# Twelve of branch four's forty filling pieces move from branch three's steps to branch four's own first six

## The reference

```
proj = h @ w_in          # queries, keys, values of all branches
o_a = diff_attention(aq, ak, av, ...)      # branches one and two of the kernel, 2 heads each
o_b = dilated_attention(bq, bk, bv, ...)   # branch three
o_c = dsa_attention(cq, ck, cv, iq, ik, iw, ...)  # branch four, keys chosen by an indexer (top 256)
x = x + concat(o_a, o_b, o_c) @ w_out
h = rmsnorm(x, norm_mem)
x = x + memory_attention(h, rmsnorm(mem, norm_memkv), w_mq, w_mkv, w_mo)
```

## Time and profile before

| | before |
|---|---|
| median of 3 runs (range) | 3524.21 us (3521.84 to 3525.72) |
| profiled execution, its span | 3520.07 us, 3518.2 us |
| PE busy, DVE busy, ACT busy | 96%, 49%, 28% |
| chain that ended last | PE 86%, DVE 7%, ACT 4% |
| steps 32 to 47 (branch three) | 192.73 us, PE busy 192.11 |
| steps 48 to 53 (branch four's first six) | 35.79 us, PE busy 24.60 |

### The profile page before, as it was taken

How to read it: one execution, slowest core, us unless ns; L and a number is a source line. 1 busy time by engine, 2 the same in 40 slices (tenths; PEclk the granted TensorE clock), 3 DMA queues, 4 the chain that set the end, 5 groups by cost and what they waited for, 6 DMA issues and landing times.

```text
span 3518.2 us, 31403 instructions
## 1 busy us (share of the span) xinstructions
PE 3361.5 (96%) x12282; PEld 1778.4 (51%) x12282; DVE 1719.0 (49%) x3098; ACT 993.8 (28%) x2083; POOL 200.2 (6%) x203
## 2 busy tenths in 40 slices
PE   7999999999989999999999899899999999999997
PEld 3466555555456444543566565664444444444443
DVE  2166191154156361551455555564345656565556
ACT  4354112002244111122477845631111000000001
POOL 0000000020000000200000000000110001111120
PEclk9999999999999999999999999899999999999999
DMA  5100121131000101111100101111000111111012
GB/s 212 59 1 13 59 90 63 54 111 35 27 7 13 35 27 54 43 34 48 42 23 32 37 19 48 67 55 42 36 12 36 48 36 58 38 42 49 35 42 72
DMA packets 52210, 163.14 MB, mean 46 GB/s; under 512 B 5552, under 2 KB 10160, under 8 KB 51389
## 3 DMA queue, kind: packets, MB, share of 16 engines
q1 hardware_dynamic: 47194, 145.23, 11.7%
q10 hardware_dynamic: 4868, 15.91, 1.3%
HBM read 156.87 MB, written 11.32 MB: 48 GB/s over the span
## 4 chain that ended last, share of the span: by engine, by line
PE 86%; DVE 7%; ACT 4%; issue 1%; SPq 1%; DMA 1%; POOL 0%; DVEq 0%; ACTq 0%; POOLq 0%
PE ps L604 25%; PE ps L634 14%; PE ps L1321 14%; PE ps L1083 6%; PE ps L762 4%; PE ps L1094 3%; PE ps L785 2%; PE ps L966 2%; PE ps L774 2%; PE ps L1106 2%; ACT sb L1863 1%; PE ps L1161 1%; PE ps L1172 1%; DVE sb L2123 1%; PE ps L1068 1%
## 5 line engine op out<-in xcount | busy, mean ns | idle before, releaser
L604 PE MATMUL ps<-sb 128*128 128x512 f32 (+1 forms) x2320 | 916.3, 555 | 13.7 <-ACT sb L1662 6.7
L1380 ACT ACTIVATE sb<-ps 128x512 f32<-128x512 f32 (+7 forms) x733 | 365.9, 515 | 1553.1 <-PE ps L604 420.5
L604 PEld LDWEIGHTS ps<-sb 128*128 128x128 f32 x2320 | 442.7, 192 | 481.3 <-issue 457.2
L634 PE MATMUL ps<-sb 128*128 128x512 f32 x1232 | 532.3, 593 | 3.6 <-ACT sb L1380 1.9
L1321 PE MATMUL ps<-sb 128*128 128x512 f32 x1232 | 530.5, 592 | 3.7 <-DVE sb L2755 3.7
L1321 PEld LDWEIGHTS ps<-sb 128*128 128x128 f32 x1232 | 233.8, 190 | 299.4 <-issue 292.3
L634 PEld LDWEIGHTS ps<-sb 128*128 128x128 f32 x1232 | 233.4, 190 | 298.3 <-issue 289.9
L1083 PE MATMUL ps<-sb 128*128 128x512 f32 x512 | 234.3, 606 | 2.4 <-DMA sb<-in_w_in 2.4
L762 PE MATMUL ps<-sb 96*128 96x512 f32 (+1 forms) x400 | 157.8, 530 | 7.1 <-ACT sb L1571 4.0
L2262 DVE SCALAR_TENSOR_TENSOR sb<-sb 128x1310 f32<-128x1310 f32 (+1 forms) x120 | 161.7, 1431 | 0.0
L1422 ACT ACTIVATE sb<-sb 128x512 f32<-128x512 f32 x128 | 74.7, 610 | 279.7 <-DVE sb L2020 119.9
(11 more groups left out here) (273 smaller groups left out, 3413.7 us busy)
## 6 DMA issues: line engine op xcount, KB each, us to landing
sb<-in_w_in SPq DMA_DIRECT2D x71, 512.0 KB, 3.3
sb<-in_w_ada SPq DMA_DIRECT2D x48, 512.0 KB, 4.4
sb<-in_w_up SPq DMA_DIRECT2D x44, 512.0 KB, 3.3
sb<-in_w_down SPq DMA_DIRECT2D x40, 256.0 KB, 2.8
sb<-in_w_out SPq DMA_DIRECT2D x16, 512.0 KB, 3.7
sb<-in_w_mkv SPq DMA_DIRECT2D x16, 512.0 KB, 3.2
rows_dram<-vec_dram ACTq DMA_DIRECT2D x1, 6906.0 KB
sb<-rows_dram ACTq DMA_DIRECT2D x6, 1024.0 KB, 5.2
```

Of the source, the lines that this page charges most:

```text
L604: ins = mm(ps[:, 0:tn], w[:, k, :], src(k, t0, tn), start=(k == 0), stop=(k == nk - 1))
L634: ins = mm(ps[:, 0:512], stationary(k), moving(k), start=(first and k == 0), stop=(k == h - 1), skip_group_check=not first)
L1380: return act(out, in_, func, scale=scale)
```

## The change

The pieces for the second tokens (c = 1) of branch four's queries and keys, eight in number, and four of its eight value tiles move from steps 32 to 47 to the twelve slots of steps 48 to 53. What stays in branch three's steps (28 pieces) is spread anew over their 32 slots, so that slots (32, 0), (36, 0), (40, 0) and (44, 0) are empty. Since weights are now used at two times, those of the four query and key blocks and the two halves of the value weights are loaded twice. H2 is read until step 53, so the memory and its square go to other places (branch three's queries and keys, QA0 and KA0), and the load of the memory waits for the scores of step 47.

```
-MEM0, KM0, VM0 = H20, H20 + 2048, H20 + 4096
+MEM0, MEMSQ0, KM0, VM0 = QA0, KA0, H20 + 2048, H20 + 4096
...
+def halves(br, order, c):
+    return [("qk", br, key, c, part) for key in order for part in range(2)]
...
-    spread(32, 48, projections(3, ("k0", "k1", "v")) + [("out", m, c) for m in range(8) for c in range(2)]
-           + projections(3, ("q0", "q1")))
-    plan[MEM_STEP, 0] = [("mem sum",)]
+    spread(32, 48, halves(3, ("k0", "k1"), 0) + [("v", 3, t) for t in range(4)]
+           + [("out", m, c) for m in range(8) for c in range(2)] + halves(3, ("q0", "q1"), 0))
+    spread(48, MEM_STEP + 2, halves(3, ("k0", "k1", "q0", "q1"), 1) + [("v", 3, t) for t in range(4, 8)])
+    plan[MEM_STEP, 0].append(("mem sum",))
...
-    mem_sq, mem_rr = km, ot2[:, 0, :]
+    mem_sq, mem_rr = view(MEMSQ0, KD, 256), ot2[:, 0, :]
...
-            if c == 0 and part == 0:
-                weights[name] = ring.take(e, "w_in2", 5 + 6 * br + i, 1024, (name, 1, "mm")).rearrange("p (k m) -> p k m", m=P)
+            if part == 0 and (c == 0 or br == 3):
+                weights[name] = ring.take(e, "w_in2", 5 + 6 * br + i, 1024, (name, c if br == 3 else 1, "mm")).rearrange(
+                    "p (k m) -> p k m", m=P)
...
-            if t == 0:
-                weights["v", br] = [ring.take(e, "w_in2", 9 + 6 * br + i, 1024, ("v2 mm", br, QT - 1)).rearrange(
+            if t == 0 or br == 3 and t == 4:
+                weights["v", br] = [ring.take(e, "w_in2", 9 + 6 * br + i, 1024, ("v2 mm", br, t + 3 if br == 3 else QT - 1)).rearrange(
...
+                e.wait_ge(*at(("s2 mm", n, 1)))
                 raw.dma_start(mem, A["mem"]).then_inc(*loads("mem_loaded", "mem"))
```

## The result

| | before | after |
|---|---|---|
| median of 4 runs each, one chip | 3524.97 us (3521.84 to 3527.03) | 3497.57 us (3494.83 to 3509.43) |
| ratio, 95% interval | | 0.9929 (0.9911 to 0.9948) |
| profiled execution, its span | 3520.07 us, 3518.2 us | 3494.83 us, 3493.0 us |
| steps 32 to 47 | 192.73 us | 154.08 us |
| steps 48 to 53 | 35.79 us | 57.83 us |

What follows compares the result with a forecast made beforehand. PE, busy 96%, was taken as the bound, with gains only where it idles or runs slowly (steps 48 to 53). -38.4 + 22.5 - 1.4 = -17.3 us from 3524.2 gave 3506.9 us, range 3500 to 3515.

Steps and rivals of the forecast that it cites:

- Branch three, -41.2 + 2.8 = -38.4: Steps 32 to 47: 41.2 us of pieces removed, 2.8 us of new waits added, 38.4 us gained.
- bank wait: Second transposes in an emptied slot wait for a bank; expected only at slot (44, 0), 0.5 us.
- the rival of less gain: Branch three shows twelve copy waits or both clock falls; gain down to 8.6 us, 3515.6; chance 0.08, or 0.02 within 7 us.
- Steps 48 to 53, 58.3 us: Filled steps last 58.3 us at full clock, against 35.8 before, so 22.5 us given back.
- the rival at half rate: Filled steps 48 to 53 stay at 1.2 GHz and last 116.6 us; total +41, 3565 us; chance 0.03.
- Step 54, 6.1 us: Step 54 falls from 7.56 to 6.1 us, a gain of 1.4 from the clock.
- The price for a fall of the clock behind the new waits: Waits for tiles 40 and 41 could drop PE to 1.2 GHz, 1.6 us each, 3.2 in all; left out of the sum.
- Loads, memory, new wait of ACT at nothing: Six added loads, the memory's load and square, and ACT's wait for step 47's scores cost no time.
- The sum, -17.3: Whole kernel: -38.4 + 22.5 - 1.4 = -17.3 us.
- How the numbers follow: Part setting the chances and the range: 3500 to 3515 us with chance 0.82; under 7 us counts as no change.
- -17.3 - 4.3 less 2 for the median's own spread, 3500: Lower bound of the range for the kernel's time, allowing 2 us for scatter of the median.
- the clock's loss in steps 48 to 53: PE's 24.60 us busy at clock 0.71 in these steps taken as about 17.5 us of work at full clock.

Runs made afterwards that it cites:

- the ranking's move: Changed kernel with the ranking pieces of tile 5 at step 45 instead of 40: 3494.77 us, ratio 0.9949 against the kernel before.
- the products that nobody reads: Kernel before plus twelve 512-column matmuls with unused results, one in each slot of steps 48 to 53: 3521.84 us, ratio 1.0010.
- the run with them alone: Kernel before with only the six added loads, the memory's new place and the wait for step 47's scores: 3514.1 us, ratio 0.9993.
- the three repeats: Changed kernel run again unchanged, against the kernel before: 3507.05, 3501.32 and 3506.97 us, ratios 0.9964, 0.9956 and 0.9959.
- eight pieces: Changed kernel with only the eight query and key pieces moved, all value tiles staying in branch three: 3511.54 us, ratio 0.9972 against before.
- slot (33, 0) filled again: Respread kernel (ranking at 45, other empty slots) with slot (40, 0) empty in place of (33, 0): 3491.73 us, ratio 0.9919 against before.

## Why the prediction was right in its steps and wrong in its range

**Branch three, -41.2 + 2.8 = -38.4.** Right: 192.73 to 154.08 is -38.65, in all four profiles of the changed kernel to 0.05 us. Steps that lost a piece and have no new wait came out 3.38 to 3.49 shorter, as worked out. The waits were 0.90 and 0.80 (forecast 1.3 and 0.9, which the prediction adds up to 2.3 instead of 2.2) and 0.56 (0.5): their places are shown by the profile, the cause of the first two by the ranking's move. Their sum, 2.26, is 0.5 us under the forecast 2.8. No further bank wait came, so the rival of less gain is out.

**Steps 48 to 53, 58.3 us.** Right: 57.83. Step by step 11.10, 8.03, 8.24, 8.68, 12.39 and 9.37 against 11.3, 8.3, 8.2, 8.7, 12.4 and 9.4. Reading a filled step off a step of branch three with the same tiles was within 0.3 us each time. The clock is 1.00; the rival at half rate (3565) is out. By the rule of the Trainium skill (TensorE: Matmul & The Clock Gate, part 1) activity releases the half rate; the trace agrees, 0.71 to 1.00 with the pieces, and 0.99 with the products that nobody reads.

**Step 54, 6.1 us.** Right: 6.13. **The price for a fall of the clock behind the new waits,** kept in the range: it did not come, steps 41 to 44 are at 1.00. Waits of 0.9 us did not bring one here; those of 1.94, 2.12 and 2.27 us in other steps and kernels did.

**Loads, memory, new wait of ACT at nothing.** Right, by the run with them alone.

**The sum, -17.3.** The stretch gave -18.04. So far nothing is off by more than 1 us.

**The step that failed** is in "How the numbers follow": "-17.3 - 4.3 less 2 for the median's own spread, 3500". The 2 us for the median's own spread were too little: they match half of the range of the three runs of before (3521.84 to 3525.72). Seventy-six single executions of the same kernel, of all later comparisons, have a standard deviation of 5.7 us and reach from 3508 to 3532 us, and 28 of the changed kernel one of 6.7, from 3494 to 3514. A median of three or four can then be off by some 5 us, and here both were, in opposite directions: that of before was high (3524.97, later 3518 to 3521), the one of after low (3497.57, later 3501 to 3507). Anchoring on three runs was part of the same mistake: against a base of 3519 the sum gives 3502. The predicted 3506.9 stands beside 3507.05, 3501.32 and 3506.97 in the three repeats, but that closeness is in part luck: the base was some 5 us too high and the gain in the total some 2 us smaller than forecast, and the two errors offset each other in part.

What the change is worth, then: the mean over all executions, the first comparison included, goes from 3518.8 us (80 of before) to 3503.9 us (28 of after), -14.9, give or take 2.8. The ratios of the repeats say the same: 0.9964, 0.9956 and 0.9959 of some 3519 us are 13 to 15.5 us. So do the profiles: from step 32 to the output projection the kernel before takes 339.3 and 336.5 us, the changed one 321.3 to 322.9 in four, which is 15.5 us in the mean. In steps 32 to 54 alone it is 18.0 against the first profile of before and 15.2 against the second. A second, smaller lesson is in that pair: the forecast took 7.1 us for the clock's loss in steps 48 to 53 off one profile (24.60 us busy, 17.5 of work), where the other shows 21.33 at 0.84, a loss of 3.4. A loss by the clock differs from one execution to the next, and one profile doesn't give its mean. The wait-filling part, 11.2 and 11.6 us idle in the two, is steady.

What stays open: whether the change moves the chance of a half-rate stretch elsewhere. PE does the same work in steps 55 to 62 before and after, with the same two long waits, of 2.35 us in step 60 and 2.47 us in step 61. All four profiles of the changed kernel have 3.4 us at half rate there. In three it lies behind the second wait, and step 61 is 1.5 us longer; in the third profile it lies behind the first, and the next wait takes it up, so that the steps last 85.95 us. Of the six other profiles with these two waits (the kernel before twice, the loads, the products that nobody reads, eight pieces, the ranking moved) none has it. Four of four against none of six would rarely be chance, but the kernel with the ranking moved differs from the changed one in branch three alone, so the change itself is not shown to be the cause. Behind step 63, too, three of the four profiles of the changed kernel last 1.5 to 3.5 us longer, with more time at half rate (1180.2 to 1182.3 us as against 1178.5 and 1178.8 in the two of before). The fall of the clock behind a wait was taken away once, with slot (33, 0) filled again, in one profile of each kernel; no experiment was made to bring one about.

## What to carry to other kernels

Fill the steps in which the matrix engine waits with independent work taken from steps in which it does not, and price the filled step by reading a full one with the same tiles. A slot whose filler seems idle may be hiding another engine's chain; look up what its next instruction waits for before emptying it. Where single executions scatter by more than the effect, compare the stretch that the edit touches, at the same granted clock, over two or more profiles, and take the base and the spread of the total from many runs; three were too few here.

## What the hardware showed that was not expected

The scatter is TensorE's clock. Over the executions of one kernel span and mean granted clock go together (correlation -0.97 for the 76 of before, and for the 28 of after), about 3 us of span for 0.001 of mean clock. Work at full clock repeats to 0.05 us; what varies is where half-rate stretches fall, each of some microseconds. Before step 32, with the same instructions in every kernel here, the twelve profiles show it: by the trace's record of the granted clock the time at half rate was 55 us in the two where step 32 began first (2008.64 and 2008.68 us), 75 in the three where it began at 2017.3 to 2018.2, and 89 in the one where it began last (2020.92). The mean clock went from 0.9844 to 0.9862 with the change: by the 3 us above, an estimate, some 5 of its 14.9 us are clock, and the rest is waits filled.

The same wait does not always bring a fall. The wait for the value product in step 61 stands in the kernel before as in the changed one, but only the changed one has 3.25 us behind it, shown above; the kernel before, PE in order of time:

```profile
2325.81 1.76 PE L1189 MATMUL ps<-sb 128*64 128x128 f32 x28 [2.46 <-ACT sb L1380]
```

And the one of 2.35 us in the changed kernel's step 60 was followed by six transposes at their usual 0.87 us in the first profile (above), but in the third by

```profile
2281.42 1.54 PE L1179 MATMUL ps<-sb 128*128 128x128 f32 x6 [2.34 <-DVE sb L2581]
```
